# Attention's products with the values: 128 moving columns instead of 64

## Chip, core and metric

The kernel runs on one core of one Trainium2 chip. The metric is the device time of one execution in microseconds (us), lower is better; the median of several runs is compared. One core has a matrix engine (TensorE, PE in the rows), a vector engine (DVE), a scalar engine (ACT), GpSimd (POOL), and a queue processor that issues most transfers (SP).

## What is computed

One decoder layer on 1024 tokens of width 1024, in float32: a norm, one input projection, two mixers side by side (sliding-window attention and a gated linear recurrence), an output projection, and a mixture of 32 experts of which each token takes four. Only the attention is touched. It has 8 query heads, 2 key-value heads and heads of 64 columns; a block of 128 queries sees its own block of keys and the one before.

```python
def sliding_window_attention(q, k, v, sinks):
    qb = q.reshape(B, nb, WINDOW, ATTN_KV_HEADS, ATTN_GROUP, ATTN_HEAD_DIM)
    kb, vb = band(k), band(v)          # previous block and this block
    scores = jnp.einsum('bnqhgd,bnkhd->bhgnqk', qb, kb) * (ATTN_HEAD_DIM ** -0.5)
    ...                                # ALiBi term, window mask, sink
    p = jnp.exp(scores - m)
    probs = p / (p.sum(axis=-1, keepdims=True) + jnp.exp(sink - m))
    out = jnp.einsum('bhgnqk,bnkhd->bnqhgd', probs.astype(dt), vb)
    return out.reshape(B, S, ATTN_WIDTH)
```

## The kernel before

Each engine has its own instruction list, written by hand, and the lists meet through semaphores. The order of stages is: turning the normed input, six units of the input projection, attention, the recurrence (four heads, one after the other), output projection and routing, then a loop over expert jobs, and a final norm. Weights are split into two parts for three fast products each; attention and the recurrence instead use plain float32 products.

Attention takes 16 steps, b = 0 to 15: block n = b // 2 and key-value head kv = b % 2, four query heads in each. TensorE's list in step b, after it has waited for the exponentials of b, is:

- the turns of step b (line 654): eight transposes of the probabilities, four for the previous block of keys and four for this one. Block 0 has no previous block, so its two steps have four;
- the scores of step b + 2 (line 634): four products with 64 rows in use, 256 moving columns each;
- a wait for the copies of the turned probabilities, then the products with the values of step b (lines 666 and 667): for each of the four query heads one product with the previous block and one with this block, added up in PSUM. The turned probabilities, 128x128, are the stationary side. The moving side is the value tile `av[:, n, ...]`, which holds 128 columns, 64 for each key-value head; 64 of them are moved.

VectorE's list in step b is: copy the turned probabilities of this block (line 1366), add up the denominator and invert it (1349, 1350), scale the finished heads of step b - 1 into `mix` (`heads_scaled`, line 1355), then for step b + 2 add the bias and mask to the scores (1337), take maxima (1340 to 1343) and so release the exponentials. ScalarE does the exponentials (984) and the copy of the previous block's turned probabilities (997). No transfer is needed by the stage. The recurrence's own products, which the prediction uses for comparison, are at lines 679 (128 moving columns), 693 (64), 710, 720 and 723 (128 each).

The trace writes each plain float32 product as two records and each transpose as one; counts of records below are counts of such entries.

Of the kernel before, what the change touches and what calls it, by code (L numbers as in the profile page):

```python
# [25 lines left out]
P = 128  # L26
# [6 lines left out]
NQ, NKV, HD = 8, 2, 64  # L33
GROUP = NQ // NKV
# [54 lines left out]
def build(nc, x, norm1_g, w_in, b_in, attn_sinks, attn_out_g, hgrn_lb_logits, hgrn_out_g, w_out,  # L89
# [6 lines left out]
    def at(name, offset, shape, dt=F32):  # L96
        return nc.alloc_sbuf_tensor_at(name, shape, dt, offset=base + int(offset))
# [23 lines left out]
    probT = at("probT", A + 48 * KB, [P, 2, GROUP, P])  # L121
# [29 lines left out]
    av = at("av", B + 68.5 * KB, [P, NT, P])  # L151
# [109 lines left out]
    with ctx:  # L261
        ps = ctx.enter_context(nc.psum_tensor("ps", [P, 8, 512], F32))
# [286 lines left out]
        def _(pe):  # L549
# [7 lines left out]
            for t in range(NT):  # L557
                pe.wait_ge(normed, t + 1)
                for half in range(2):
                    i = 2 * t + half  # L560
                    if i >= 8:
                        pe.wait_ge(turned_lo, i - 7)
                    for k in range(4):
                        m = pe.transpose(ps[:, i % 8, k * P:(k + 1) * P],
                                         xs[:, t, (4 * half + k) * P:(4 * half + k + 1) * P], ident[:, :])
# [62 lines left out]
            def scores(b):  # L628
                n, kv = divmod(b, 2)
                if b >= 2:  # L630
                    pe.wait_ge(score_added, b - 1)
                lo = P if n == 0 else 0
                for i in range(GROUP):
                    m = pe.matmul(ps[:, 2 * kv + i // 2, (i % 2) * 256 + lo:(i % 2) * 256 + 256],  # L634
                                  aq[64 * kv:64 * kv + 64, i, n * P:(n + 1) * P],
                                  ak[64 * kv:64 * kv + 64, n * P + lo:n * P + 256],
                                  start=True, stop=True)
                m.then_inc(scored, 1)
# [3 lines left out]
            for b in range(2 * NT):  # L642
                n, kv = divmod(b, 2)

                pe.wait_ge(exped, b + 1)
                if b >= 1:
                    pe.wait_ge(pT_act, b)
                    pe.wait_ge(pT_dve, b)
                for half in range(2):
                    if n == 0 and half == 0:  # L650
                        pe.sem_inc(probs_turned, 1)
                        continue
                    for i in range(GROUP):
                        m = pe.transpose(ps[:, 4 + half, i * P:(i + 1) * P],  # L654
                                         score[:, kv, i, half * P:half * P + P], ident[:, :])
                    m.then_inc(probs_turned, 1)
                if b + 2 < 2 * NT:
                    scores(b + 2)
                pe.wait_ge(pT_act, b + 1)
                pe.wait_ge(pT_dve, b + 1)  # L660
                if b >= 2:
                    pe.wait_ge(heads_out, b - 1)
                for i in range(GROUP):
                    o = ps[:, 6 + kv, i * HD:(i + 1) * HD]
                    if n > 0:
                        pe.matmul(o, probT[:, 0, i, :], av[:, n - 1, kv * HD:kv * HD + HD], start=True, stop=False)  # L666
                    m = pe.matmul(o, probT[:, 1, i, :], av[:, n, kv * HD:kv * HD + HD], start=n == 0, stop=True)  # L667
                m.then_inc(heads_done, 1)


# [1 line left out]
            for hd in range(HH):  # L672
# [5 lines left out]
                for t in range(NT):  # L678
                    m = pe.matmul(ps[:, 2 + t // 4, (t % 4) * P:(t % 4 + 1) * P],
                                  hk[:, hd, t * P:(t + 1) * P], hq[:, hd, t * P:(t + 1) * P],  # L680
                                  start=True, stop=True)
                m.then_inc(diag_done, 1)
                for L in range(LEVELS):
# [7 lines left out]
                    for t in range(NT):  # L691
                        v = hp[:, s % 2, t * P:(t + 1) * P]
                        m = pe.matmul(ps[:, lev % 2, t * 64:(t + 1) * 64], v,  # L693
                                      v.rearrange("p (m two h) -> p m two h", two=2, h=h)[:, :, 1, :],
                                      start=True, stop=True)
# [6 lines left out]
                for t in range(NT):  # L702
                    m = pe.transpose(ps[:, 4 + t // 4, (t % 4) * P:(t % 4 + 1) * P],
                                     hp[:, s % 2, t * P:(t + 1) * P], ident[:, :])
# [4 lines left out]
                for t in range(NT - 1):  # L709
                    m = pe.matmul(ps[:, 6 + t // 4, (t % 4) * P:(t % 4 + 1) * P], kbT[:, t, :],  # L710
                                  hv[:, t, hd * P:(hd + 1) * P], start=True, stop=True)
# [6 lines left out]
                for t in range(NT):  # L718
                    o = ps[:, 2 + t // 4, (t % 4) * P:(t % 4 + 1) * P]
                    m = pe.matmul(o, attT[hd % 2][:, t, :], hv[:, t, hd * P:(hd + 1) * P],  # L720
                                  start=True, stop=t == 0)
                    if t > 0:
                        m = pe.matmul(o, hp[:, s % 2, t * P:(t + 1) * P], state[:, t - 1, :],
                                      start=False, stop=True)
# [509 lines left out]
        def _(dve):  # L1234
# [33 lines left out]
            for t in range(NT + 1):  # L1268
# [17 lines left out]
                if t >= 1:  # L1286
                    for half in range(2):
                        i = 2 * (t - 1) + half
# [63 lines left out]
            def heads_scaled(b):  # L1352
                n, kv = divmod(b, 2)
                dve.wait_ge(heads_done, b + 1)
                dve.tensor_tensor(mix[:, n, kv * 256:kv * 256 + 256].rearrange("p (i d) -> p i d", i=GROUP),
                                  ps[:, 6 + kv, 0:256].rearrange("p (i d) -> p i d", i=GROUP),
                                  stat[:, 5, b, :].unsqueeze(2).broadcast_to([P, GROUP, HD]),
                                  ALU.mult).then_inc(heads_out, 1)

# [2 lines left out]
            for b in range(2 * NT):  # L1362
                dve.wait_ge(probs_turned, 2 * b + 2)
                if b >= 1:
                    dve.wait_ge(heads_done, b)
                dve.tensor_copy(probT[:, 1, :, :], ps[:, 5, :].rearrange("p (i n) -> p i n", i=GROUP)).then_inc(pT_dve, 1)
                denominator(b)
                if b >= 1:
                    heads_scaled(b - 1)
                if b + 2 < 2 * NT:  # L1370
                    add_bias(b + 2)
            heads_scaled(2 * NT - 1)


# [521 lines left out]
```

## Time and profile before

| | |
|---|---|
| median of 3 runs | 2513.24 us (2499.37 to 2523.63) |
| the profiled execution | 2511.87 us, of which the span is 2510.3 us |
| TensorE busy (matmul) | 2262.9 us, 90% of the span |
| VectorE / ScalarE / GpSimd busy | 1595.8 / 1359.9 / 468.7 us |
| mean granted clock of TensorE | 0.91 of full speed |
| attention's steps in the trace | from 319 us to 453 us of the span |

The page's busy time says which engine is used most over the whole run. The table of 40 slices shows where the granted clock is below full speed. The chain of work that ended last shows, stretch by stretch, which engine set the pace.

### The profile page before, as it was taken

The page shows a single profiled execution, that of the slowest core. Times are in us where ns is not written, and L with a number is a line of the kernel's source. Part 1 is how long each engine was busy: PE and PEld are TensorE (multiplying, and loading weights), DVE is VectorE, ACT ScalarE, POOL GpSimd, SP SyncE. Part 2 cuts the span into 40 slices and gives each one's busy share as a digit, 9 for nine tenths or more (in the row PEclk, how much of TensorE's full clock was granted, in tenths as well). Part 3 has the DMA queues.
Part 4 walks back from the last instruction along what each step waited for, and adds up shares of the span by engine and source line. Part 5 has one row for each costly group of instructions (what it writes and reads, how often), then busy time and mean ns, then how long its engine had stood idle before and what let it go on. Part 6 is the DMA issues. An engine that isn't in the chain of part 4 may idle for free.

```text
span 2510.3 us, 38622 instructions
## 1 busy us (share of the span) xinstructions
PE 2262.9 (90%) x10494; PEld 1881.0 (75%) x10495; DVE 1595.8 (64%) x2261; ACT 1359.9 (54%) x2036; POOL 468.7 (19%) x478
## 2 busy tenths in 40 slices
PE   5999899678797599999999999999999999999992
PEld 4888778677686487877878778787877878778781
DVE  4121254767455577777677776778677777776774
ACT  5211232433232567667576665767666676665764
POOL 3000000223013112121131111312121131211310
PEclk7999955566897799999999999999999999999996
DMA  5111200000321889798897987979797897987976
GB/s 170 39 43 58 74 4 1 10 17 9 107 82 62 279 254 297 220 321 268 255 306 237 300 281 230 312 245 362 220 330 254 267 305 228 314 274 242 314 238 237
DMA packets 260586, 506.15 MB, mean 202 GB/s; under 512 B 34282, under 2 KB 35307, under 8 KB 260369
## 3 DMA queue, kind: packets, MB, share of 16 engines
q1 hardware_dynamic: 241874, 456.02, 54.1%
q0 software_dynamic: 18656, 49.45, 8.4%
q8 instruction: 30, 0.49, 0.1%
q14 instruction: 22, 0.17, 0.0%
q10 hardware_dynamic: 4, 0.02, 0.0%
HBM read 466.24 MB, written 39.17 MB: 201 GB/s over the span
## 4 chain that ended last, share of the span: by engine, by line
PE 67%; DMA 13%; DVE 8%; issue 7%; ACT 4%; DVEq 1%; ACTq 1%; SPq 1%; POOLq 0%; POOL 0%
PE ps L551 13%; PE ps L553 13%; PE ps L552 13%; DMA raw<-in_w 12%; PE ps L880 6%; PE ps L881 6%; PE ps L820 2%; DVE wlo L1610 2%; PE ps L873 2%; PE ps L634 2%; PE ps L693 2%; PE ps L840 1%; PE ps L667 1%; PE ps L666 1%; PE ps L654 1%
## 5 line engine op out<-in xcount | busy, mean ns | idle before, releaser
L1610 DVE TENSOR_TENSOR wlo<-raw,whi 128x1024 fp32r<-128x1024 f32 x774 | 927.1, 1216 | 83.0 <-ACT whi L1110 64.5
L1110 ACT ACTIVATE whi<-raw 128x1024 fp32r<-128x1024 f32 x775 | 809.4, 1057 | 251.1 <-PE ps L881 126.2
L551 PE MATMUL ps<-whi,xTh 128*128 128x512 f32 x1024 | 405.7, 396 | 0.0
L552 PE MATMUL ps<-wlo,xTh 128*128 128x512 f32 x1024 | 400.8, 391 | 0.0
L553 PE MATMUL ps<-whi,xTl 128*128 128x512 f32 x1024 | 400.5, 391 | 0.0
L1850 POOL DMA_INDIRECT acc_d<-y,icur x64 | 114.4, 1787 | 1046.2 <-ACT y L1152 1036.6
L553 PEld LDWEIGHTS ps<-whi,xTl 128*128 128x128 f32 x1024 | 192.8, 188 | 41.4
L552 PEld LDWEIGHTS ps<-wlo,xTh 128*128 128x128 f32 x1024 | 193.1, 189 | 40.0
L551 PEld LDWEIGHTS ps<-whi,xTh 128*128 128x128 f32 x1024 | 193.0, 188 | 38.7
L551 PE MATMUL ps<-whi,aTh 128*128 128x512 f32 x512 | 216.8, 423 | 0.5 <-DVE aTl L1654 0.5
L553 PE MATMUL ps<-whi,aTl 128*128 128x512 f32 x512 | 203.8, 398 | 0.0
L552 PE MATMUL ps<-wlo,aTh 128*128 128x512 f32 x512 | 202.9, 396 | 0.0
L880 PE MATMUL ps<-whi,xTh 128*128 128x512 f32 x480 | 187.3, 390 | 0.0
L881 PE MATMUL ps<-wlo,xTh 128*128 128x512 f32 x480 | 187.2, 390 | 0.0
L873 PE MATMUL ps<-brow,ones 128*128 128x512 f32 x282 | 117.5, 417 | 56.4 <-ACT sig L1137 42.9
L1116 ACT ACTIVATE xTh<-ps 128x512 fp32r<-128x512 f32 (+1 forms) x132 | 64.8, 491 | 135.0 <-PE ps L820 134.6
L1261 DVE TENSOR_TENSOR wlo<-raw,whi 128x1024 fp32r<-128x1024 f32 (+1 forms) x24 | 27.3, 1136 | 171.5 <-ACT whi L922 171.2
L1646 DVE TENSOR_SCALAR lin<-ps 128x256 f32<-128x256 f32 x128 | 53.9, 421 | 111.8 <-PE ps L881 111.0
L553 PEld LDWEIGHTS ps<-whi,aTl 128*128 128x128 f32 x512 | 97.5, 190 | 22.3
L873 PEld LDWEIGHTS ps<-brow,ones 128*128 128x128 f32 x282 | 53.2, 189 | 76.4 <-issue 63.7
L552 PEld LDWEIGHTS ps<-wlo,aTh 128*128 128x128 f32 x512 | 98.2, 192 | 16.1
L551 PEld LDWEIGHTS ps<-whi,aTh 128*128 128x128 f32 x512 | 97.9, 191 | 14.8 <-DVE wlo L1610 0.8
(285 smaller groups left out, 4044.5 us busy)
## 6 DMA issues: line engine op xcount, KB each, us to landing
raw<-in_w SPq DMA_DIRECT2D x776, 512.0 KB, 6.4
raw<-in_w_in SPq DMA_DIRECT2D x16, 512.0 KB, 3.6
xs<-in_x SPq DMA_DIRECT2D x8, 512.0 KB, 8.0
raw<-in_w_out SPq DMA_DIRECT2D x8, 512.0 KB, 3.7
mix<-in_x SPq DMA_DIRECT2D x8, 512.0 KB, 4.2
acc_d<-mix SPq DMA_DIRECT2D x8, 512.0 KB, 5.1
h_d<-h SPq DMA_DIRECT2D x8, 512.0 KB, 3.1
mix<-acc_d SPq DMA_DIRECT2D x8, 512.0 KB, 6.5
```

The source lines that it names most:

```text
L551: pe.matmul(o, sh, mh_, start=start, stop=False, skip_group_check=skip)
L552: pe.matmul(o, sh, ml_, start=False, stop=False, skip_group_check=skip)
L553: return pe.matmul(o, sl, mh_, start=False, stop=stop, skip_group_check=skip)
L634: m = pe.matmul(ps[:, 2 * kv + i // 2, (i % 2) * 256 + lo:(i % 2) * 256 + 256], aq[64 * kv:64 * kv + 64, i, n * P:(n + 1) * P], ak[64 * kv ...
L873: pe.matmul(o, (ones2, ones1)[b][:, :], brow[:, bias:bias + UNIT], start=True, stop=False)
L880: pe.matmul(o, sh[:, k, 1, :], wh[:, a, :], start=False, stop=False)
L881: m = pe.matmul(o, sh[:, k, 1, :], wl[:, a, :], start=False, stop=last)
L1110: act.activation(slot(whis, s), slot(raws, s), ACT.Copy).then_inc(split_hi, 1)
L1116: act.activation(xTh[:, 4 * half:4 * half + 4, b, 0:n], ps[:, 6 + half, :].rearrange("p (k n) -> p k n", k=4)[:, :, 0:n], ACT.Copy).then_i ...
L1610: dve.tensor_tensor(slot(wlos, s), slot(raws, s), slot(whis, s).bitcast(F32), ALU.subtract).then_inc(split_lo, 1)
L1646: dve.tensor_scalar(lin[0:n, b, :], hid[:, :, 1], 1.0 + LIMIT, 1.0 - LIMIT, ALU.min, ALU.max).then_inc((hid_taken[0], lin_set)[b], 1)
L1850: pool.indirect_dma_start(out=acc_d, out_offset=bass.IndirectOffsetOnAxis(ap=icur[0:n, b:b + 1], axis=0), in_=y[0:n, b, :], in_offset=None ...
```

## The change

The moving side of both products becomes the whole value tile, 128 columns, so that each product also computes the 64 columns of the other key-value head. Its result takes 128 columns of PSUM instead of 64; four of them fill the bank of 512 columns that belonged to this kv already. `heads_scaled` reads the 64 columns of its own head out of each 128. The transposes, the scores, all waits and all orders stay.

```diff
                 for i in range(GROUP):
-                    o = ps[:, 6 + kv, i * HD:(i + 1) * HD]
+                    o = ps[:, 6 + kv, i * P:(i + 1) * P]
                     if n > 0:
-                        pe.matmul(o, probT[:, 0, i, :], av[:, n - 1, kv * HD:kv * HD + HD], start=True, stop=False)
-                    m = pe.matmul(o, probT[:, 1, i, :], av[:, n, kv * HD:kv * HD + HD], start=n == 0, stop=True)
+                        pe.matmul(o, probT[:, 0, i, :], av[:, n - 1, :], start=True, stop=False)
+                    m = pe.matmul(o, probT[:, 1, i, :], av[:, n, :], start=n == 0, stop=True)
                 m.then_inc(heads_done, 1)
...
                 dve.tensor_tensor(mix[:, n, kv * 256:kv * 256 + 256].rearrange("p (i d) -> p i d", i=GROUP),
-                                  ps[:, 6 + kv, 0:256].rearrange("p (i d) -> p i d", i=GROUP),
+                                  ps[:, 6 + kv, :].rearrange("p (i d) -> p i d", i=GROUP)[:, :, kv * HD:kv * HD + HD],
                                   stat[:, 5, b, :].unsqueeze(2).broadcast_to([P, GROUP, HD]),
                                   ALU.mult).then_inc(heads_out, 1)
```

## Rows read from the trace of the kernel before

**Rows 1.** Busy time by stretch, core 0; after each engine its records, then granted clock.

```profile
core 0: us, PE busy (x) PEld busy (x) DVE busy (x) ACT busy (x) POOL busy (x), PEclk, DMA share, GB/s
350.00:370.00 20.00, 20.00 (x73) 16.59 (x72) 8.69 (x19) 7.26 (x30) 0.00 (x0) 0.50 0.00 0
390.00:410.00 20.00, 20.00 (x71) 16.18 (x70) 8.90 (x19) 5.31 (x20) 0.00 (x0) 0.50 0.00 1
```

**Rows 2.** Chain that ended last, step b = 11: start us, us, engine, tile, line, records.

```profile
413.07 1.71 PE ps L654 x8
414.77 3.71 PE ps L634 x8
418.48 0.62 PE ps L666 x2
419.10 0.43 PE ps L667 x2
...
422.09 1.71 PE ps L654 x8
```

**Rows 3.** Groups by line and form, 300 to 460 us: busy us, mean ns.

```profile
L634 PE MATMUL ps<-ak,aq 64*128 64x256 f32 x112 | 52.9, 651 | 0.0
L667 PE MATMUL ps<-av,probT 128*128 128x64 f32 x128 | 39.5, 422 | 0.0
L666 PE MATMUL ps<-av,probT 128*128 128x64 f32 x112 | 36.2, 427 | 1.7 <-ACT probT L997 0.8 <-issue 0.8
```

**Rows 4.** Chain that ended last, products of the recurrence with 128 moving columns.

```profile
509.51 0.43 PE ps L720 x2
...
511.14 0.22 PE ps L720 x2
```

**Rows 5.** Busy time by stretch in the recurrence; columns as in rows 1.

```profile
459.60:463.10 3.50, 3.50 (x16) 3.46 (x16) 3.50 (x2) 2.23 (x2) 0.00 (x0) 0.50 0.00 0
463.10:466.50 3.40, 0.22 (x2) 0.00 (x0) 3.40 (x3) 0.00 (x0) 0.00 (x0) 0.99 0.00 0
474.00:486.00 12.00, 12.00 (x57) 11.89 (x56) 10.88 (x16) 3.17 (x3) 3.81 (x3) 0.50 0.00 0
500.70:504.10 3.40, 3.31 (x14) 3.06 (x14) 3.19 (x5) 1.09 (x2) 1.27 (x1) 0.50 0.00 0
504.20:507.40 3.20, 0.00 (x0) 0.00 (x0) 2.99 (x9) 1.06 (x1) 0.00 (x0) 1.00 0.00 0
507.80:510.90 3.10, 3.00 (x14) 3.03 (x15) 1.29 (x2) 0.00 (x0) 0.00 (x0) 0.50 0.00 0
514.30:517.70 3.40, 3.40 (x32) 3.40 (x32) 1.23 (x1) 1.53 (x5) 0.55 (x1) 1.00 0.41 152
517.80:521.10 3.30, 1.87 (x17) 1.73 (x16) 2.89 (x5) 0.61 (x1) 1.27 (x1) 1.00 0.00 0
521.30:524.50 3.20, 3.20 (x16) 3.20 (x16) 2.99 (x4) 1.38 (x6) 1.26 (x1) 0.50 0.00 0
542.70:546.00 3.30, 3.07 (x14) 2.77 (x13) 3.08 (x3) 0.86 (x1) 1.27 (x1) 0.50 0.00 0
546.00:549.00 3.00, 0.00 (x0) 0.00 (x0) 2.79 (x9) 1.06 (x1) 0.00 (x0) 0.50 0.00 0
```

**Rows 6.** Instructions in order of time, one step: start us, busy us, engine, line.

```profile
387.75 0.69 DVE L1366 COPY probT<-ps 128x512 f32<-128x512 f32 x1 [2.26 <-PE ps L654]
...
388.76 0.42 DVE L1355 TENSOR_TENSOR mix<-ps,stat 128x256 f32<-128x256 f32 x1
...
391.46 1.23 DVE L1337 TENSOR_TENSOR score<-ps,alibi 128x1024 f32<-128x1024 f32 x1 [2.28 <-PE ps L634]
...
394.61 0.51 ACT L984 ACTIVATE score<-score,stat 128x256 f32<-128x256 f32 x1 [6.37 <-DVEq L1344]
```

**Rows 7.** Chain that ended last, the stage's last two steps; columns as in rows 2.

```profile
431.11 1.71 PE ps L654 x8
...
436.56 1.24 DVE score L1337
...
442.66 0.66 PE ps L666 x2
...
446.31 1.71 PE ps L654 x8
448.02 0.83 issue
448.85 0.66 PE ps L666 x2
...
452.53 0.42 DVE mix L1355
```

## The prediction

> **What bounds the kernel now.** I began with the page's busy times and its 40 slices, to find where the change lies and how the clock stands there, and then took the attention stage apart: busy time by stretch, the chain that ended last, and the groups by line. The reader is to see three things. First, TensorE is busy 20.00 of 20 us in the middle of the stage, and yet its granted clock is 0.50, the lower level, 1.2 GHz [rows 1]. Second, the chain runs through TensorE alone, step after step: eight turns 1.71 us, eight records of scores 3.71 us, sixteen records of products with the values (0.62 us for the first two, 0.43 us for each of the seven pairs after that, 3.6 us), and the next step starts 422.09 - 413.07 = 9.02 us later [rows 2]. Third, VectorE is busy only 8.7 to 8.9 of those 20 us and the transfer share is nil [rows 1]. So the stage is bound by TensorE at half clock, and whatever speeds TensorE up here shortens the run until VectorE binds.
>
> **The cost of the wider products.** There are 112 + 128 = 240 records of them [rows 3]. With 64 moving columns a pair takes 0.43 us at the low clock [rows 2]. The recurrence has the same product with 128 moving columns and the same 128x128 stationary side, and its pair takes 0.43 us too, at the low clock, and 0.22 us at the high one [rows 4]. So at 64 columns something other than the moving of columns sets the 0.21 us of a record, and 128 just fit beside it. Cost at an unchanged clock: 240 x 0 = 0 us. The lower bound is 0 as well (nothing in the change makes a record shorter at the same clock). The upper bound, if the fit failed and time went with the columns, would be 240 x 0.213 = 51 us; the row at 128 columns is the nearest possible, so I take 0.
>
> The Trainium skill (TensorE: Matmul & The Clock Gate, section "Back-to-back issue gap") gives N / 1.2 ns for a matmul of N columns at the low clock, which is 53 and 107 ns here; by that rule the change would add an estimated 240 x 53 ns = 13 us. The trace disagrees for this form, since records of 64 and 128 columns both stand at 0.21 us, and the measurement decides.
>
> **VectorE's side.** `heads_scaled` still reads 128x256 elements, now in runs of 64 out of 128, and took 0.42 us, sixteen times [rows 6]. A strided read from the same bank could cost nothing or, at the very most, as much as reading all 512 columns: the copy of 128x512 out of PSUM takes 0.69 us [rows 6], so 0 to 0.27 us per step. It lies in the part of VectorE's list that runs while TensorE does scores. I take 0; if VectorE binds (below), the bound is 16 x 0.27 = 4 us.
>
> **What the change can do to the clock.** This is where I expect the time. The recurrence shows what precedes a rise. Sixteen records of full 128-column products (459.6 to 463.1) ended with the clock at 0.99 from 463.1 on; fourteen of them (500.7 to 504.1) ended with 1.00 at 504.2, when the engine was already idle; after the next such run, from 507.8, it was high again. Against that, 57 records in 12 us with 64 moving columns, back to back and 12.00 of 12 us busy, left it at 0.50 [rows 5]. So busy time is not what tells the two cases apart; the engine's work within it is. Attention before the change is of the second kind: its products move 64 columns in the time of 128, and its scores use 64 rows of the 128 [rows 3]. After the change each step has an unbroken run of sixteen 128-column records, 3.4 us at low clock, followed at once by eight turns of 128 columns, 1.7 us: 5.1 us, longer than the runs that raised it in the recurrence. One such run did not raise it: fourteen records in 542.7 to 546.0 with an idle engine behind them, still 0.50 after [rows 5]. Three of the four such runs shown did, and here there is no idle time on either side, and thirteen tries. I expect the clock to be up by the first or second step that has sixteen records.
>
> Will it stay up? With the high clock the level products stayed at 1.00 through 514.3 to 517.7 although they move 64 columns, since at high clock there are twice as many in the same time, and it fell only after a stretch in which the engine worked 1.87 of 3.30 us on such products [rows 5]. Attention at high clock would have TensorE nearly always busy, with half of its time on full-width work, so I expect it to hold.
>
> **The sum.** At high clock a step of TensorE is 1.71 / 2 + 3.71 / 2 + (0.2 + 16 x 0.11) = 0.86 + 1.86 + 1.96 = 4.7 us [rows 2, 4]. VectorE's step does not depend on that clock: from the copy to the end of `heads_scaled` 387.75 to 389.18 is 1.43 us, and from the bias to the release of the exponentials 391.46 to 394.6 is 3.15 us [rows 6], 4.6 us in all. Its waits for TensorE (2.26 and 2.28 us in these rows) close up: scores end 1.86 us after the turns, when VectorE has just finished its 1.43 us. The two engines come out nearly equal; with handovers I take 4.8 us, a gain of 9.02 - 4.8 = 4.2 us a step.
>
> Steps b = 2 to 13 begin 9.02 us apart, the last of them at 431.11 us [rows 2, 7]. If the first run of sixteen (that of b = 2) raises the clock, b = 3 to 12 are short: 10 x 4.2 = 42 us. The last two steps are a chain of another kind: turns and scores of step 13, 1.71 + 3.71 us; then bias, maxima, exponentials and copy, 436.56 to 442.66 = 6.1 us on VectorE and ScalarE, unchanged; then products 3.65, turns 1.71, a wait of 0.83, products 3.65 us [rows 7]. The first part halves for 2.7 us. Of the 6.1 us TensorE would fill 2.8 and idle 3.3, and the clock may be lost there; the rest gains between 0 and (3.65 + 1.71 + 3.65) / 2 = 4.5 us. I take 2.2, so 5 us for the tail. Sum: 42 + 5 = 47 us off the profiled execution's 2511.9, which is 2465 us. That execution is 1.4 us below the median of the runs shown, so the forecast against the median is the same 2465, a ratio of 0.981.
>
> Behind the stage everything comes earlier together; the next work is VectorE's, on the recurrence's gates, and a high clock finds nothing to speed up there. The expert loop starts 47 us sooner and is unchanged; no transfer that it needs is started in this stage. Only the clock's ups and downs in the recurrence may fall differently; a high stretch there, as that from 514.3 to 521.1 [rows 5], is worth about half its length, 3 us either way.
>
> **The rivals.**
>
> *The clock goes up and down.* The scores use half the rows; if they hardly count towards keeping the clock, one step is fast and the next slow. For it: 517.8 to 521.1 [rows 5], where it fell with the engine still working. Against it: at high clock scores are only 1.86 us between full-width work. Half of the gain: 21 + 3 = 24 us, so 2488 us.
>
> *The clock never rises in the stage.* Then the wider products cost nothing and bring nothing: 2512 us. For it: the run of 542.7 to 546.0 that raised nothing, and TensorE's busy time, which is complete already at 0.50 [rows 1]. Against it: three rises after just such products, and the longer runs here. The Trainium skill (same page, section "What's actually happening") says that a gate before the array is throttled by default and that activity releases it. Read as the engine's busy time, that rule would make the change do nothing, since busy time cannot grow; the stretches of rows 5 speak against that reading, as both kinds in it are fully busy.
>
> *The columns cost time* (the other sign). If a record of the products went from 0.213 to 0.427 us, 240 x 0.213 = 51 us are added at low clock: 2563 us. It decides as soon as the record is longer than 0.23 us without a rise of the clock. Against it stands the pair of 0.43 us at 128 columns [rows 4].
>
> *It rises earlier.* Step 1's eight products and step 2's turns are 3.4 us of full-width work, so b = 2 may be partly fast, and TensorE and VectorE may overlap at 4.6 us a step with a fast tail: 44 + 7 + 4 = 55 us, 2457 us. I count it with the forecast.
>
> **How the numbers follow.** Clock up and held, with the early variant: 0.60, between 2450 and 2475. Up and down: 0.18, 2475 to 2496. Never up: 0.14, 2500 to 2523. Columns cost: 0.04, about 2563. Something not seen: 0.04, on either side. A range of 2449 to 2495 holds the first case and nearly all of the second, 0.77, and the runs of before spread by 12 us around their median, which its ends allow for. The first case's own range is 2450 to 2475. About 1% (25 us) is what a measurement of this kernel can tell from no change. Faster by over 1% (below 2488): the first case and most of the second, 0.60 + 0.13 + 0.02 = 0.75. Within 1%: the rest of the second and the third, 0.19. Slower: 0.06.
>
> **What would show it.** In the profile after: the granted clock between 345 us and the end of the stage at 1.00; line 666 and 667 pairs at 0.22 us; steps about 4.8 us apart; the waits of lines 1366 and 1337 for TensorE nearly gone; the stage ended near 406 us instead of 453. While the clock is still low, pairs of 0.43 us; if they are 0.85 us, the price was wrong. If the clock row is 0.50 throughout, the mechanism is wrong; if it alternates, only its hold is. If the clock is high and steps stay far above 4.8 us, the handovers between TensorE and VectorE were mis-sized.

## The result

The changed kernel takes 2477.09 us (median of 4 executions, 2469.54 to 2481.01) beside 2512.03 us for the kernel before (median of 4, 2499.37 to 2523.63). The ratio is 0.9863, with a 95% interval of 0.9829 to 0.9896: 35 us, 1.4% faster. A repetition with six executions of the changed kernel gave 2478.61 beside 2516.08 us, ratio 0.9868 (0.9823 to 0.9913). The forecast was 2465 us, with a range of 2449 to 2495. The ratios here and below leave out executions that are more than 1.5% above the fastest of their kernel.

The profiled execution of the changed kernel took 2476.75 us, 35.1 us less than that of before. The busy time by stretch answers to rows 1 and shows the mechanism at once (columns as there: each engine's busy time and records, then the granted clock, transfer share, GB/s):

```profile
core 0: us, PE busy (x) PEld busy (x) DVE busy (x) ACT busy (x) POOL busy (x), PEclk, DMA share, GB/s
306.00:330.00 24.00, 16.32 (x57) 12.99 (x58) 16.40 (x36) 8.76 (x31) 1.08 (x2) 0.50 0.12 44
331.00:346.00 15.00, 13.12 (x86) 10.90 (x85) 11.90 (x26) 7.95 (x30) 0.00 (x0) 1.00 0.01 2
...
378.00:394.00 16.00, 14.42 (x97) 12.19 (x97) 12.52 (x28) 7.95 (x30) 0.00 (x0) 1.00 0.00 1
```

Before, the clock stood at 0.50 through the whole stage and TensorE was busy for every microsecond of its middle. After, it is 1.00 from 330.5 to 398.8 us, TensorE is busy for 87 to 90% of that time, and VectorE, once busy for 44% of the time, for 78%. So TensorE alone no longer sets the pace. The chain of work that ended last shows the same steps as rows 2 with everything at the high clock, and with other engines in between (start us, us, engine, tile, line, records):

```profile
367.14 0.22 PE ps L667 x2
367.36 0.22 PE ps L666 x2
...
368.26 0.87 PE ps L654 x8
369.13 1.93 PE ps L634 x8
371.09 1.24 DVE score L1337
372.46 1.23 DVE stat L1340
374.28 0.37 issue
374.65 1.66 ACT score L984 x7
376.41 0.49 ACT probT L997
376.94 0.49 PE ps L666 x2
...
378.99 0.87 PE ps L654 x8
379.87 1.94 PE ps L634 x8
```

A pair of 128-column records takes 0.22 us, eight turns 0.87, scores 1.93. From the turns at 368.26 to the turns at 378.99 is 10.73 us, and that is two steps, not one: 5.37 us a step, where it was 9.02. Where the clock is low in the same trace, a pair of 128 columns takes 0.43 us, exactly what a pair of 64 took (this is the first half of step 14, again from the chain):

```profile
398.89 0.43 PE ps L667 x2
399.33 0.43 PE ps L666 x2
```

`heads_scaled` takes 424 ns in the median, as before.

### The profile page after: what moved, and what is told of

The parts are those of the page before. It is cut to its first block, busy times and chain, and to the rows that moved or that the text cites. A ratio compares the mean times of both kernels' runs of the same rounds, so it can differ in the third digit from the quotient of the medians.

```text
span 2475.1 us, 38622 instructions
## 1 busy us (share of the span) xinstructions
PE 2217.1 (90%) x10494; PEld 1844.5 (75%) x10495; DVE 1595.8 (64%) x2261; ACT 1359.5 (55%) x2036; POOL 468.6 (19%) x478
## 4 chain that ended last, share of the span: by engine, by line
PE 65%; DMA 13%; DVE 8%; issue 7%; ACT 5%; DVEq 1%; ACTq 1%; SPq 1%; POOLq 0%; POOL 0%
PE ps L551 13%; PE ps L553 13%; PE ps L552 13%; DMA raw<-in_w 12%; PE ps L880 6%; PE ps L881 6%; PE ps L820 2%; PE ps L873 2%; DVE wlo L1610 2%; PE ps L693 2%; PE ps L840 1%; ACT whi L1110 1%; PE ps L634 1%; ACT yfold L1156 1%; ACT y L1152 1%
## 5 line engine op out<-in xcount | busy, mean ns | idle before, releaser
L1646 DVE TENSOR_SCALAR lin<-ps 128x256 f32<-128x256 f32 x128 | 53.7, 420 | 112.0 <-PE ps L881 111.0
L873 PEld LDWEIGHTS ps<-brow,ones 128*128 128x128 f32 x282 | 53.7, 190 | 78.2 <-issue 58.2
```

The source lines that it names most:

```text
L873: pe.matmul(o, (ones2, ones1)[b][:, :], brow[:, bias:bias + UNIT], start=True, stop=False)
L1646: dve.tensor_scalar(lin[0:n, b, :], hid[:, :, 1], 1.0 + LIMIT, 1.0 - LIMIT, ALU.min, ALU.max).then_inc((hid_taken[0], lin_set)[b], 1)
```

## The experiments

The stage's length below is read from each trace, from the first turns (line 654) to the end of the last product with the values (line 667). "Clock high" is for how long of it the granted clock was 1.00. The usual step is the mean of two where long and short ones alternate.

| kernel | stage, us | clock high, us | usual step, us | median of the kernel |
|---|---|---|---|---|
| before, four traces | 133.8, 120.5, 126.8, 133.8 | 0, 20, 10, 0 | 9.02 | 2512 to 2516 |
| changed, three traces | 89.0, 94.2, 88.8 | 72, 64, 75 | 5.37 | 2477, 2479; the third trace a single 2486.35 |
| e1, ScalarE's order | 79.5 | 68 | 4.78 | 2466.5 |
| e2, 96 columns | 88.7 | 71 | 5.36 | 2482.5 |
| e3, 64 rows | 125.2 | 0 | 9.02 and 7.48 | (other jobs) |
| e5, before with e1's order | 114.2 | 27 | 9.02, then 4.73 | 2500.4 |
| e6, before with paired scores | 105.2 | 48 | 6.9 | 2492.6 |
| e7, wide, order and paired | 78.8 | 68 | 4.61 | 2473.4 |
| e8, wide in steps 0 to 3 only, order | 82.8 | 63 | 4.73 | 2468.7 |

The executions without a kept trace agree on the clock. Its mean over the whole execution was 0.901 to 0.923 in the 37 executions of the kernel before that were timed beside the experiments, and 0.925 to 0.936 in all eleven of the changed kernel.

**What raises the clock: columns (e2) and rows (e3).** The theory is that the full-width work of the products raises the clock. The first run moves 96 columns instead of 128:

```diff
-                    o = ps[:, 6 + kv, i * P:(i + 1) * P]
+                    o = ps[:, 6 + kv, i * P:i * P + 96]
...
-                        pe.matmul(o, probT[:, 0, i, :], av[:, n - 1, :], ...)
+                        pe.matmul(o, probT[:, 0, i, :], av[:, n - 1, 32 * kv:32 * kv + 96], ...)
...
```

> The changed kernel with 96 moving columns instead of 128 in both products with the values (the needed 64 and 32 of the other head). Theory A: what raises the clock is the engine's work inside its busy time, and 96 columns lie between the two kernels: records still take 0.21 us at low clock, and the clock comes up during the stage, perhaps later and with falls back to 0.50: between 2477 and 2500 us. Rival B: it depends on some property that only whole tiles of 128 have (the reach over all columns, the bank filled): the clock stays at 0.50 through the stage as before the change, 2512 us.

Measured: 2482.5 us (4 executions, 2474.53 to 2484.45), ratio 0.9888 (0.9831 to 0.9946). The clock rose at 332.6 us, as soon as in the changed kernel (330.5, 340.6 and 324.2 us in its three traces), and stayed until 400.9:

```profile
306.00:330.00 24.00, 14.74 (x50) 11.39 (x51) 15.11 (x35) 9.35 (x32) 1.08 (x2) 0.50 0.16 58
334.00:399.00 65.00, 56.88 (x381) 48.02 (x379) 50.83 (x110) 32.56 (x124) 0.00 (x0) 1.00 0.00 1
```

So no whole tile of 128 is needed; rival B falls. The later rise and the falls that theory A thought possible did not come either. The second run keeps the 128 columns and uses 64 rows:

```diff
-                        pe.matmul(o, probT[:, 0, i, :], av[:, n - 1, :], ...)
-                    m = pe.matmul(o, probT[:, 1, i, :], av[:, n, :], ...)
+                        pe.matmul(o, probT[0:64, 0, i, :], av[0:64, n - 1, :], ...)
+                    m = pe.matmul(o, probT[0:64, 1, i, :], av[0:64, n, :], ...)
```

> The changed kernel with 128 moving columns, but only 64 rows on both sides of the products with the values: 64 of each block's 128 keys are left out of the products, so the numbers are not the reference's. Records take the same time at the same clock. Theory A: rows in use count as columns do, as the scores with 64 rows did not raise the clock before: the clock stays at 0.50 in the stage, about 2512 us, like the kernel before. Rival B: only the columns moved count: the clock rises as in the changed kernel, about 2477 us.

In the stage theory A held: the clock was 0.50 throughout, with TensorE busy 107 of 110 us. This is one trace, and the kernel before has such executions too; but all seven traces with 96 or 128 columns and full rows (changed, e1, e2, e7, e8) had the high clock by 340.6 us, and the mean clock of e3's four executions, 0.902 to 0.915, is like that of the kernel before (a weaker sign, since the loop differs as well, as told next).

```profile
330.00:440.00 110.00, 107.15 (x419) 92.12 (x416) 55.24 (x118) 35.80 (x134) 0.00 (x0) 0.50 0.00 1
```

Its whole time, 2466.3 us, says nothing on the stage: the altered attention sends tokens to other experts, and the expert loop had 7013 matmul records instead of 7233 and was 1593 us long instead of 1632. I had not thought of that when I forecast a whole time for it. Only its stage is used here. The stage is also shorter than expected, 125.2 us, because every second step took 7.48 us; this came unexpected and is told below.

**Why the step is 5.37 and not 4.8 us (e1).** The chain above goes from ScalarE's exponentials (line 984) through its copy (line 997) to the products. In the changed kernel's timeline the exponentials of step b + 2 stand in ScalarE's list ahead of the copy for step b + 1, so that copy, and TensorE behind it, waits for scores made two steps ahead. The edit puts the copy first:

```diff
             exps(0)
             exps(1)
+            exps(2)
             for b in range(2 * NT):
...
-                if b + 2 < 2 * NT:
-                    exps(b + 2)
+                if 3 <= b + 1 < 2 * NT:
+                    exps(b + 1)
```

> The changed kernel with one order edited in ScalarE's list: the copy of the turned probabilities of step b (line 997) now stands ahead of the exponentials of step b + 1 or later, instead of behind those of step b + 1 and ahead of b + 2's; each step's exponentials come right after the copy of the step before. Theory A: the changed kernel's step of 5.37 us (10.73 us for two) is set by a loop in which the copy waits behind the next but one exponentials; with it gone, VectorE's own 4.6 us binds, so a step takes 4.6 to 4.8 us, some 8 us less over the stage, and the products no longer wait 0.8 us for line 997: 2468 to 2471 us. Rival B: the step is set by VectorE and TensorE waiting for each other in turn (copy after turns, bias after scores), whatever ScalarE does: step stays at 5.3 us and the time at 2477 us.

Measured: 2466.53 us (6 executions, 2461.83 to 2480.32), ratio 0.9834 (0.9785 to 0.9883). The usual step is 4.78 us and the stage 79.5 us against 89.0, although the edit makes step 0 longer, 10.01 us instead of 6.59, because `exps(2)` now stands in ScalarE's list ahead of the release of step 0's products. The chain is now TensorE alone again:

```profile
360.45 0.87 PE ps L654 x8
361.32 1.92 PE ps L634 x8
363.24 0.42 PE ps L666 x2
363.66 0.22 PE ps L667 x2
...
365.22 0.87 PE ps L654 x8
```

365.22 - 360.45 = 4.77 us. The step and its cause came as theory A said, but the engine that binds is not VectorE: TensorE's 0.87 + 1.92 + 0.42 + 7 x 0.22 = 4.77 us is a little more than VectorE's 4.6, and between 340 and 388 us TensorE is busy 48.00 of 48 us. The kernel's median lies 1.5 us below the range of theory A. It also lies 12 us below the changed kernel's in the same comparison; its stage is 11.2 us shorter than the mean of the changed kernel's three (90.7 us). The executions of the two kernels overlap in time, so it is the stage in the trace that shows the gain.

**Is the order worth something by itself (e5)?** The same edit on the kernel before, with 64 columns.

> The kernel before (64 moving columns) with only the order of ScalarE's list edited as in e1. Theory A: at the low clock TensorE alone sets the step, so the order is worth nothing there: steps stay at 9.02 us, the last two gain some 2 us because the products of step 14 no longer wait behind the exponentials of step 15: 2510 to 2516 us against 2516. Rival B: the order was what counted in e1 at any clock: steps get shorter here too and the time falls by 8 us or more.

Neither expectation held as a whole. The median was 2500.41 us (ratio 0.9906, 0.9867 to 0.9946), 12.5 us less than before, which is more than the 8 of rival B, while the steps at low clock stayed at 9.02 us as theory A said. Its ten executions ran from 2471.95 to 2520.61, a spread of 49 us, where nineteen executions of the kernel before spread over 24. The trace shows what can make such a spread. The clock stays low for 95.6 us, until 398.0, with steps of 9.02 us. Then it rises with nothing changed in the work, and stays high for 27 us:

```profile
320.00:397.00 77.00, 73.65 (x260) 60.43 (x259) 36.47 (x77) 20.72 (x79) 0.00 (x0) 0.50 0.00 1
398.50:424.00 25.50, 24.20 (x168) 20.83 (x167) 21.80 (x49) 15.00 (x55) 0.00 (x0) 1.00 0.01 1
```

So with 64 columns, too, the clock can come up, late or early by luck, and with ScalarE's order mended a step is then 4.73 us. The fastest execution, 2471.95 us, is as fast as the wide kernels and has their mean clock, 0.933; that the clock came early in its stage is likely but not shown, as no trace of it was kept.

**How typical was the trace of before? (three repetitions)**

> The kernel before once more, unedited, for a second trace. The expert loop, from the first turns of a job to the last scatter, took 1632 us in its first trace and 1638 to 1649 us in the four traces of kernels that start it some 45 us earlier. Theory A: chance of single executions; here it takes between 1630 and 1650 us. Rival B: the earlier start costs the loop some 10 us; here it takes 1632 us again.

> The kernel before, unedited, third trace. It is to show how often the stage of 133.8 us of the first trace stands for the kernel, and how often the clock comes up in it, as in the second trace (120.5 us, high for 20 us). Theory A (the clock's luck explains why the gain was 36 and not 47 us): most executions of before lie between these. Rival B: the first trace is typical and the second an exception.

> The kernel before, unedited, fourth trace; as the third. Also for the loop: its length goes so far with the number of short drops of the clock in it, 1632 and 1635 us with five, up to 1649 with twelve. Theory A: the kernel before too comes out with more than five drops now and then, and is then 2 us longer for each. Rival B: five belong to the kernel before, and more to an earlier start.

Their single times were 2499.94, 2514.26 and 2525.62 us. In the second trace the clock was high for 20 us of the stage, in the third for 10, in the fourth never. Of the second:

```profile
366.00:386.00 20.00, 20.00 (x75) 16.82 (x74) 8.44 (x19) 7.13 (x27) 0.00 (x0) 0.50 0.00 1
387.00:406.00 19.00, 16.33 (x110) 13.76 (x108) 15.16 (x33) 7.96 (x30) 0.00 (x0) 1.00 0.00 1
```

The mean of the four stages is 128.7 us, not 133.8. The expectation for the third said that most would lie between the first two. The third does; the fourth is as long as the first, so with two of four at 133.8 us the rival, that the first is typical, is only half refuted. What is shown is that the clock comes up by itself in some executions.

The three rises with 64 columns that were traced (386.2 and 413.9 us here, 398.0 in e5) came at the same place of a step: after sixteen records of products and eight turns without a pause, as the last of the turns ended. This is the one at 386.2 (start us, us):

```profile
383.95 0.63 PE L667 MATMUL ps<-av,probT 128*128 128x64 f32 x2
384.38 1.91 PE L654 MATMUL ps<-ident,score 128*128 128x128 f32 x8
386.22 1.13 PE L634 MATMUL ps<-ak,aq 64*128 64x256 f32 x4
```

**Raising and holding (e8).** Wide products in steps 0 to 3 only, 64 columns in the twelve steps after, on e1's kernel:

```diff
+                cols = slice(0, P) if b < 4 else slice(kv * HD, kv * HD + HD)
+                wd = cols.stop - cols.start
                 for i in range(GROUP):
-                    o = ps[:, 6 + kv, i * P:(i + 1) * P]
+                    o = ps[:, 6 + kv, i * wd:(i + 1) * wd]
...
```

> e1's kernel with 128 moving columns only in steps 0 to 3 and 64 again in steps 4 to 15; ScalarE's order of e1 stays. The second trace of the kernel before and that of e5 showed the clock high for 20 to 27 us of the stage with 64 columns only. Theory A: full-width products are needed to raise the clock early and surely, but once it is high, with TensorE nearly always busy, 64 columns hold it: steps of 4.7 to 4.8 us after the first four, 2464 to 2470 us like e1. Rival B: narrow products don't hold it for long: it falls during steps 4 to 15 and steps go back to 9.02 us: 2480 to 2505 us.

Measured: 2468.65 us (4 executions, 2459.82 to 2476.15), ratio 0.9826 (0.9777 to 0.9874), the same as e1 within what can be told. The clock rose at 337.1 us and stayed at 1.00 through all twelve narrow steps:

```profile
337.50:352.00 14.50, 14.50 (x99) 12.46 (x98) 11.93 (x25) 7.26 (x27) 0.00 (x0) 1.00 0.00 1
352.00:400.00 48.00, 45.88 (x323) 39.73 (x322) 39.59 (x89) 28.93 (x104) 0.00 (x0) 1.00 0.00 1
```

Theory A held: with the width the rise comes early, by 340.6 us in seven traces of seven, and without it at 386.2 us or later or not at all, in five of five (four of before, e5). For the hold the width was not needed in this one trace, in which TensorE had hardly a pause (45.9 of 48 us busy). In the second trace of before, with ScalarE's old order and TensorE busy 16.3 of 19 us, narrow products held it for 20 us only. And in the changed kernel, which keeps the old order, two of the three traces have a short drop in the middle of the stage. The order alone does not explain the drops, since e7 has the new order and one too, at 375.5 us, after TensorE was busy 36.2 of 45 us. This is the one of the second trace:

```profile
341.00:381.00 40.00, 35.58 (x233) 30.08 (x232) 31.83 (x68) 19.26 (x74) 0.00 (x0) 1.00 0.00 1
382.00:385.00 3.00, 3.00 (x16) 3.00 (x16) 1.28 (x4) 1.56 (x7) 0.00 (x0) 0.50 0.01 3
386.00:405.00 19.00, 14.86 (x102) 12.72 (x102) 13.60 (x31) 8.05 (x31) 0.00 (x0) 1.00 0.01 1
```

**Scores of both heads side by side (e6, e7).** e3's short steps suggested that products in different halves of the rows run at the same time. In e6 the kernel before issues the scores of both key-value heads alternately, every second step:

```diff
-            def scores(b):
-                n, kv = divmod(b, 2)
+            def scores(b):
+                n = b // 2
                 if b >= 2:
-                    pe.wait_ge(score_added, b - 1)
+                    pe.wait_ge(score_added, b)
                 lo = P if n == 0 else 0
                 for i in range(GROUP):
-                    m = pe.matmul(...)
-                m.then_inc(scored, 1)
+                    for kv in range(NKV):
+                        m = pe.matmul(...)
+                        if i == GROUP - 1:
+                            m.then_inc(scored, 1)
...
-            scores(1)
...
-                if b + 2 < 2 * NT:
+                if b + 2 < 2 * NT and kv == 0:
```

> The kernel before (64 moving columns) with the scores of both key-value heads issued alternately, eight products of 64 rows every second step: head 0 uses rows 0 to 63, head 1 rows 64 to 127. In e3 a step whose scores and products lay in different halves of the rows took 7.48 us instead of 9.02. Theory A: products in different row halves run at the same time, so two steps cost 3.7 us of scores instead of 7.4: 14.3 us for two steps instead of 18.0, some 24 us off, if the clock stays at 0.50: 2492 us. If both halves together also raise the clock, 2470 us. Rival B: what e3 showed is something else (the shorter stationary load): 2516 us.

Measured: 2492.61 us (10 executions, 2487.88 to 2500.18), ratio 0.9931 (0.9907 to 0.9954). The time is that of theory A, but the reason is mixed: the clock went up and down, 0.74 on average between 320 and 420 us. Both parts can be seen in the timeline, where sixteen records of scores, two steps' worth, take 2.58 us. The products right behind them are at the high clock, those of the next step, after a wait of 3.08 us for ScalarE's copy, at the low one (a line edited in moved the numbers by one):

```profile
370.09 2.58 PE L635 MATMUL ps<-ak,aq 64*128 64x256 f32 x16
372.60 0.43 PE L667 MATMUL ps<-av,probT 128*128 128x64 f32 x2
...
378.56 0.69 PE L667 MATMUL ps<-av,probT 128*128 128x64 f32 x2 [3.08 <-ACT probT L998]
379.04 0.63 PE L668 MATMUL ps<-av,probT 128*128 128x64 f32 x2
```

e7 puts all three edits together:

> Three edits together: 128 moving columns, ScalarE's order of e1, and the paired scores of e6. Theory A: VectorE's 4.6 to 4.8 us a step binds at high clock, so TensorE's shorter step brings nothing there; only the first steps, before the clock is up, gain: 2460 to 2467 us, as e1 within what can be told. Rival B: the handovers bind rather than VectorE's own work, and a shorter TensorE step shows: steps below 4.7 us and a time under 2458 us.

Measured: 2473.43 us (4 executions, 2466.84 to 2482.74), ratio 0.9868 (0.9823 to 0.9913). The step goes down from 4.78 to 4.61 us on average (4.78 and 4.44 in turn), which is what VectorE's list takes, and the stage is 78.8 us against 79.5. Its whole time lies above the stated range and is not better than e1's. With TensorE's step shortened VectorE binds: it works through its list with no wait for another engine, one copy 4.61 us after the other, so there is nothing more to be had from TensorE here.

```profile
350.91 0.69 DVE L1368 COPY probT<-ps 128x512 f32<-128x512 f32 x1 [0.22 <-DVE stat L1345]
...
355.52 0.69 DVE L1368 COPY probT<-ps 128x512 f32<-128x512 f32 x1 [0.22 <-DVE stat L1345]
```

**Where the rest of the gain went (e4 and a third trace of the changed kernel).**

> The changed kernel once more, unedited, for a second trace of it and a tighter ratio. Its first trace ended the attention stage 46.7 us earlier than the kernel before, but the whole execution only 35.1 us; the other 11.6 us were lost in the expert loop, where its clock dropped in 10 short stretches against 5. Theory A: that is chance of that pair of executions (where the clock's ups and downs fall against the jobs), so here the loop's length differs again and the ratio lies between 0.980 and 0.987. Rival B: the earlier start costs the loop something lasting: the loop again takes 1617 us against 1608 and the ratio stays at 0.986.

> The changed kernel, unedited, third trace: its stage took 89.0 and 94.2 us so far, its loop 1643 and 1649 us with 9 and 12 drops of the clock. Theory A (chance): stage 88 to 96 us, and the loop anywhere between 1632 and 1650, by the number of its drops. Rival B (lasting): loop again 1643 us or more.

The second and third traces of the changed kernel had stages of 94.2 and 88.8 us; its mean over three is 90.7 us, 38.0 us less than the mean of before. The medians differ by 34.9 and 37.5 us. The expert loop, from the first turns of gathered tokens to the last scatter, took 1631.7, 1635.0, 1643.0 and 1641.1 us in the four traces of before (mean 1637.7) and 1642.9, 1648.9 and 1650.6 in the three of the changed kernel (mean 1647.5). In the four other wide kernels that start the loop as early (e1, e2, e7, e8) it took 1641.8, 1637.7, 1642.9 and 1638.8. Its length goes with the time at low clock in it: 31.8 and 34.1 us in the two shortest, 62.8 and 63.4 us in the two longest. Over the thirteen traces of kernels that run the same jobs (all but e3) a line through them gives 0.49 us of loop for each microsecond at low clock, and the loops lie within 3 us of it. So the difference goes with the clock; why the clock drops more often in one execution than in another is not shown. On the loop theory A fared badly: both repetitions of the changed kernel came out long, 1648.9 and 1650.6 us, as rival B said. But the sharp form of B, that five drops belong to the kernel before, is out (its third trace has nine in 1643.0 us), and e1, e2, e7 and e8 speak against a fixed price of an early start. That the three loops of the changed kernel all lie at the upper end stays open. Part of it belongs to the executions that were traced: these three took 2482.6 us on average, while the median of the ten executions in the two comparisons is 2477.1. With 38.0 us gained in the stage and 35 to 37.5 us in the medians, at most some 3 us are left for the loop and all else.

## Why the prediction was right, and where it was off

**The cost of the wider products: 0 us.** Right. The pair is 0.43 us at low clock and 0.22 at high, for 64, 96 and 128 columns alike. What sets it, if not the columns, was not tested. The estimate from the Trainium skill's rule on the gap between matmuls (TensorE: Matmul & The Clock Gate, "Back-to-back issue gap"), 13 us more, did not come.

**VectorE's strided read: 0 us.** Right, 424 ns as in rows 6.

**The clock rises after one or two runs of full-width products.** Right in kind and, in two of three traces, earlier than forecast. In the first the clock rose at 330.5 us, after the eight-record products of step 1 and with the turns of step 2 under way; this was the variant "it rises earlier". In the third it rose at 324.2 us, after the eight records of step 0 and with the turns of step 1 under way, which no case foresaw. In the second it rose at 340.6, after step 2's sixteen records, as forecast. To the comparison of rows 5 the runs add that 96 columns over 128 rows brought the rise at 332.6 us (e2), and that 128 columns over 64 rows did not bring it in 125 us (e3). The Trainium skill's sentence that activity releases the throttle (same page, "What's actually happening") fits only if activity is read as work in the array; e3's 107 busy microseconds of 110 at 0.50 rule out the other reading.

**It stays up.** Right for the stage as a whole, with one short drop in the middle of it in two of three traces, and one in the pause of the last two steps in all three. The rivals "up and down" and "never rises" fell for the changed kernel; "up and down" describes e6.

**The step: 4.8 us forecast, 5.37 measured.** This term was mis-sized, by 0.57 us a step. The working counted TensorE's and VectorE's lists and the waits between these two, and left ScalarE's list out, because ScalarE is busy for half of the step only. What binds is not its work but the place of one copy in its list. Shown by e1: with that place mended the step is 4.78 us. VectorE's waits for TensorE ahead of lines 1366 and 1337 were to be nearly gone; in the first trace 12.0 and 9.7 us are left, of 32.9 and 31.8 before, and TensorE's products wait 9.8 us for the copy of line 997. Between the turns of steps 3 and 13 the first trace gained 90.2 - 53.7 = 36.5 us instead of 42; the early rise gave 3.0 back in step 2.

**The tail: 5 us forecast, 5.3 measured** (from the turns of step 13 to the end of the last product, 21.6 before and 16.3 after). The clock was lost in the pause and came back for the last products, the middle of the two bounds.

**From the stage to the whole: the step that was furthest off.** In the profiled pair the stage ended 46.7 us earlier, which is the sum of the forecast, 47, by some luck (2.0 us of it are an earlier start of the stage). But the sum was made against one execution of before and then set equal to the median's change. The kernel before has executions in which the clock comes up in the stage by itself: its mean stage is 128.7 us and not 133.8, which takes 5 us off the gain. That the first execution as a whole still lay at the median was luck of its own: its loop, 1631.7 us, is the shortest of the four, 6 us below their mean. The slow step and the occasional drop take the rest: 90.7 us for the mean stage against the 86.8 that the forecast implies, another 4 us. That leaves 38 of 47 us, and the medians show 35 and 37.5. The range held because it reached to the case of half the gain.

## What to carry to other kernels

Where a profile shows TensorE fully busy at half clock, look at what its instructions use of the array, not at its busy time: short products whose record is as long as that of wider ones can be widened for nothing, as the 64 and 128 columns here, and it may be enough to do so at the start of a stage and to keep the engine free of pauses after. When a bound is lifted, read every engine's list in order for what stands ahead of the instruction that the next step needs, also on an engine that is only half busy. And before a forecast from one execution is set against a median, ask which events in it are luck; here the clock's rise in the kernel before was one.

## What was not expected of the hardware

**Products in different halves of the rows overlap.** In e3, where the products with the values use rows 0 to 63, every second step took 7.48 us instead of 9.02. Its timeline shows records of scores (of the head in rows 64 to 127) between the products, both at their full length:

```profile
376.42 0.79 PE L666 MATMUL ps<-av,probT 64*128 64x128 f32 x2
376.84 0.63 PE L634 MATMUL ps<-ak,aq 64*128 64x256 f32 x1
377.00 0.63 PE L667 MATMUL ps<-av,probT 64*128 64x128 f32 x2
377.26 0.63 PE L634 MATMUL ps<-ak,aq 64*128 64x256 f32 x1
```

In e6, sixteen such records of scores in alternate halves, those at 370.09 us, took 2.58 us with the clock high for part of it, where sixteen one after the other take 7.4 us at low clock and 3.9 at high. The Trainium skill (TensorEngine Tiling (Array Packing), section "Key Properties") states that tiles of the array, here two of 64 rows, can execute loads and matmuls in parallel, and these traces agree; that an ordinary kernel gets this from the order of its products alone, I had not expected.

The overlap also goes with the clock. In e6 it first rose at 320.1 us, before any product with the values, while sixteen records of scores in alternate halves ran:

```profile
316.97 1.09 PE L655 MATMUL ps<-ident,score 128*128 128x128 f32 x4 [7.20 <-ACT score L985]
317.99 3.03 PE L635 MATMUL ps<-ak,aq 64*128 64x256 f32 x16
320.95 1.10 PE L668 MATMUL ps<-av,probT 128*128 128x64 f32 x8
```

In the four traces of the kernel before, with the scores of one head at a time, it never rose before 386.2 us.

**The clock's rise is not a fixed property of an instruction stream.** In the kernel before the clock fell ahead of the stage, at 304 to 306 us. In two executions it then stood at 0.50 for 157 us, over the whole stage, and in two others it rose 82 and 109 us after that fall, with the same steps of 9.02 us and TensorE fully busy before the rise. The traces show at which place of a step it rose, as told above; what decides in which execution it does was not tried.
